# One core, hybrid attention model: order of loads, high parts and low parts around the exchange of the streamed operand in the last stage

## Chip, cores and metric

The kernel runs as one program on one core of a Trainium2 chip. The metric is the time of one execution on the device in microseconds, over several runs. Engines are named as in the profile: PE (matrix multiply), ACT (scalar), DVE (vector), POOL (GpSimd), SP (the queue that issues most of the transfers).

## What is computed

The reference is two blocks one after the other on a sequence of 1024 tokens with 1024 channels: the first with window attention, a bidirectional mLSTM and a mixture of experts, the second with an even and an odd layer and a last RMS norm. The change touches only the end of the odd layer and that norm:

```python
def odd_layer(x, norm_g, w_in, conv_w, w_out):
    ...
    y_c = y_c.reshape(Bn, S, C_WIDTH) * jax.nn.silu(g_c)
    y_d = short_gated_conv(d_b, d_c, d_x, conv_w) * jax.nn.silu(g_d)
    return x + jnp.concatenate([y_c, y_d], axis=-1) @ w_out
...
    return rmsnorm_2(h, final_norm)
```

The last product is y (1024 tokens x 2048) by w_out (2048 x 1024), in float32. The kernel splits each float32 operand into a high part (a cast to the matmul's format) and a low part (the rest), and adds three products of them.

## The kernel before

**Stages.** The stages follow one another in one program; each gives each engine its instructions in a fixed order, and an engine works them off in that order. Semaphores carry the dependences. The odd layer is phase_odd.

**Pairs and products.** The odd layer's projections and the last product run in *pairs* m: two tiles of 128 weight columns by 1024 channels against the tokens, done by a scheme with seven half-size products in place of eight (class Quarters). Product i of pair m is 12 matmuls: 4 slices of the contraction by high x high, high x low, low x high, each 128 x 128 by 512 columns. Pairs 0 to 39 serve the attention heads, 40 to 55 the convolution (PAIRS = 56), and 56 to 63 the last product. There the roles turn: the pieces of y are what is loaded as stationary weights (quarter_raw, quarter_hi, quarter_lo), and w_out is the operand that streams (odd_t_sum raw, odd_t_hi, odd_t_lo), seven pieces of 1 MB each. Four of the seven are sums that the kernel has made beforehand and stored (last_w_sums). Pairs 56 to 59 take chunk 0 of w_out, pairs 60 to 63 chunk 1. So the seven streamed pieces are exchanged twice, while pair 55 gives way to pair 56 and pair 59 to pair 60. Piece i can be overwritten once product i of the pair before is through.

**Who does what.** SP loads: four quarters of the weights of each pair (Quarters.load, part 0 three of them, part 1 the last; each waits until POOL has used the buffer), the operand's pieces (load_operand, waits for product i of the last pair of the chunk before), tiles of x (load_x), and it stores the rows of the result. POOL makes for each pair four sums of quarters and seven low parts, in the order sum 1, 2, 3, low 0 to 3, sum 4, low 4 to 6 (Quarters.pool, lines 3009, 3012, 3013, 3020 and 3002). ACT makes the high parts of the weights, four products ahead: hi(m, i) makes that of product 7m + i + 4 (line 2996), so hi(m, 2) is the one of (m, 6) and hi(m, 3) that of (m+1, 0). ACT also copies products 0, 1, 2 and 6 of a pair out of PSUM (copy, line 3106; for chunk 1 DVE does that, add, line 4991), and makes the operand's high parts (operand_hi, line 4445). DVE joins products 3, 4 and 5 to what was copied (join, line 3112) and makes the operand's low parts (operand_lo, line 4940).

**What PE waits for.** Quarters.multiply makes PE wait for the low part of the weights of that product, and besides:

```python
                if i == 2:
                    pe.wait_ge(self.copied, 4 * m + 1)
                if i == 3 and m >= 2:
                    pe.wait_ge(self.joined, 3 * (m - 2) + 3)
                if i == 4:
                    pe.wait_ge(self.copied, 4 * m + 3)
                if i == 6:
                    pe.wait_ge(self.joined, 3 * (m - 1) + 2)
```

So product 4 waits for the copy of product 2, and product 6 for the join of product 4. In pairs 56 and 60 each product waits for its operand low part too.

**The norm.** In pairs 61 to 63 the rows of the pair before are finished beside the products: ACT sums the squares, DVE makes the mean (mean), ACT the root (root), DVE the inverse and the scaling, SP the store. add_x adds the turned x.

## Time and profile before

| | us |
|---|---|
| median of 3 runs | 3244.09 |
| lowest, highest | 3243.22, 3247.24 |
| the profiled execution, its own time | 3243.6 |
| its span, first to last instruction | 3241.9 |
| mean granted clock of PE, share of full speed | 0.984 |

One execution was recorded by the hardware profiler. A row of a timeline gives start and length of an instruction in microseconds from the start of the span, and in brackets how long its engine sat idle before it and what released it ("issue" where the profile shows no releaser). The start of a matmul is measured and its end is modelled, so matmuls that follow one another overlap in the rows; the pace is read from start to start. The last stage, pairs 56 to 63, takes the last 180 us of the span.

### The profile page before, as it was taken

Reading aid. Unit: us, or ns where it says so; the run is one execution under the profiler, and the core shown is the slowest. Engines: PE = TensorE matmul, PEld = TensorE weight load, DVE = VectorE, ACT = ScalarE, POOL = GpSimd, SP = SyncE. Lnnn points to the kernel's source line nnn. Section 1 sums busy time; section 2 is a strip of 40 time slices with the busy share of each in tenths; the row PEclk is TensorE's granted clock in tenths of the full one; section 3 lists DMA queues with packets and bytes.
Section 4 is the critical chain, followed back from the end, with each engine's and each line's share of the span. In section 5 each row is a group of like instructions: output and inputs, shape, how many; then the busy total and the mean of one; then the engine's idle time right before and its main releaser. Section 6 shows DMA issues by size and latency. Waiting matters only on the chain. (4 is left out here: it accounts for less than half of the span.)

```text
span 3241.9 us, 43876 instructions
## 1 busy us (share of the span) xinstructions
PE 3104.1 (96%) x16242; PEld 2572.7 (79%) x16242; DVE 1707.5 (53%) x2457; ACT 1452.3 (45%) x2457; POOL 1683.6 (52%) x1096
## 2 busy tenths in 40 slices
PE   6989999889899989999999999999999999999998
PEld 4777887866788868788888788888888888888777
DVE  5366633854799876622523744444444444467544
ACT  5156313723677743333401555445455445333443
POOL 2331323042322249976643656556556556689886
PEclk8999999999899989999999999999999999999999
DMA  8230212173999952222432111111111111244553
GB/s 297 56 86 21 57 40 75 44 260 119 337 400 394 375 166 69 78 98 62 155 101 80 40 47 52 46 53 46 46 56 43 47 56 43 89 146 162 169 173 106
DMA packets 341492, 388.12 MB, mean 120 GB/s; under 512 B 29367, under 2 KB 297563, under 8 KB 335012
## 3 DMA queue, kind: packets, MB, share of 16 engines
q1 hardware_dynamic: 329374, 344.39, 31.7%
q0 software_dynamic: 4896, 16.78, 2.0%
q10 hardware_dynamic: 7014, 24.17, 1.9%
q8 instruction: 131, 2.15, 0.3%
q14 instruction: 77, 0.63, 0.1%
HBM read 313.73 MB, written 68.16 MB: 118 GB/s over the span
## 5 line engine op out<-in xcount | busy, mean ns | idle before, releaser
L3002 POOL TENSOR_TENSOR quarter_lo<-quarter_w_sums,quarter_hi 128x512 fp32r<-128x512 f32 x325 | 470.5, 1455 | 244.5 <-ACT quarter_hi L2996 242.1
L3002 POOL TENSOR_TENSOR quarter_lo<-quarter_raw,quarter_hi 128x512 fp32r<-128x512 f32 x244 | 355.0, 1455 | 280.2 <-ACT quarter_hi L2996 273.2
L3092 PE MATMUL odd_z<-odd_t_hi,quarter_hi 128*128 128x512 f32 x876 | 362.4, 414 | 4.3 <-POOL quarter_lo L3002 3.8
L2996 ACT CAST quarter_hi<-quarter_w_sums 128x512 fp32r<-128x512 f32 x325 | 202.4, 623 | 362.9 <-PE first_z L3094 172.5
L3092 PE MATMUL first_z<-odd_t_hi,quarter_hi 128*128 128x512 f32 x868 | 358.8, 413 | 6.1 <-issue 4.8
L3094 PE MATMUL odd_z<-odd_t_hi,quarter_lo 128*128 128x512 f32 x876 | 343.6, 392 | 0.0
L3093 PE MATMUL odd_z<-odd_t_lo,quarter_hi 128*128 128x512 f32 x876 | 342.1, 391 | 0.0
L3094 PE MATMUL first_z<-odd_t_hi,quarter_lo 128*128 128x512 f32 x868 | 339.8, 391 | 0.0
L3093 PE MATMUL first_z<-odd_t_lo,quarter_hi 128*128 128x512 f32 x868 | 338.3, 390 | 0.0
L2996 ACT CAST quarter_hi<-quarter_raw 128x512 fp32r<-128x512 f32 x244 | 151.5, 621 | 120.7 <-PE first_z L3094 55.8
L276 POOL TENSOR_TENSOR w_hi<-w_raw,zero_col 128x1024 fp32r<-128x1024 f32 x25 | 49.7, 1990 | 288.1 <-DMA w_raw<-in_w_in 98.0
L3092 PEld LDWEIGHTS odd_z<-odd_t_hi,quarter_hi 128*128 128x128 f32 x876 | 165.2, 189 | 36.7 <-POOL quarter_lo L3002 4.7
L3092 PEld LDWEIGHTS first_z<-odd_t_hi,quarter_hi 128*128 128x128 f32 x868 | 163.3, 188 | 38.1 <-issue 9.1
L3094 PEld LDWEIGHTS odd_z<-odd_t_hi,quarter_lo 128*128 128x128 f32 x876 | 164.8, 188 | 36.2
L3094 PEld LDWEIGHTS first_z<-odd_t_hi,quarter_lo 128*128 128x128 f32 x868 | 162.8, 188 | 35.8
L3093 PEld LDWEIGHTS odd_z<-odd_t_lo,quarter_hi 128*128 128x128 f32 x876 | 165.4, 189 | 30.1
L3093 PEld LDWEIGHTS first_z<-odd_t_lo,quarter_hi 128*128 128x128 f32 x868 | 163.6, 188 | 29.4
L4755 DVE SCALAR_TENSOR_TENSOR dil_biased<-const,odd_aux 128x128 f32<-128x128 f32 (+1 forms) x192 | 78.0, 406 | 192.4 <-PE odd_aux L4268 122.6
L3106 ACT ACTIVATE dil_set<-odd_z 128x512 f32<-128x512 f32 x112 | 90.7, 810 | 175.0 <-PE odd_z L3094 175.0
L3106 ACT ACTIVATE dil_set<-first_z 128x512 f32<-128x512 f32 x108 | 88.3, 818 | 166.6 <-PE first_z L3094 166.6
L4775 DVE COPY dil_p_t<-odd_aux 128x128 f32<-128x128 f32 (+1 forms) x192 | 67.7, 353 | 171.7 <-PE odd_aux L4285 151.7
L3009 POOL TENSOR_TENSOR quarter_w_sums<-quarter_raw 128x512 f32<-128x512 f32 x82 | 119.6, 1458 | 28.6 <-POOL quarter_lo L3002 13.3
(716 smaller groups left out, 7790.2 us busy)
## 6 DMA issues: line engine op xcount, KB each, us to landing
quarter_raw<-in_odd_w_in SPq DMA_DIRECT2D x224, 256.0 KB, 3.5
raw_gate<-in_w_gate SPq DMA_DIRECT2D x16, 2048.0 KB, 15.7
raw_up<-in_w_up SPq DMA_DIRECT2D x16, 2048.0 KB, 15.8
raw_down<-in_w_down SPq DMA_DIRECT2D x16, 2048.0 KB, 15.5
quarter_raw<-in_even_w_in SPq DMA_DIRECT2D x64, 256.0 KB, 3.3
start_w_mod<-in_w_mod SPq DMA_DIRECT2D x11, 1024.0 KB, 10.8
w_raw<-in_w_in SPq DMA_DIRECT2D x16, 512.0 KB, 3.8
mix_w_early<-in_w_mod SPq DMA_DIRECT2D x8, 1024.0 KB, 12.0
```

The source lines that it names most:

```text
L276: pool.tensor_tensor(w_hi[:, u], w_raw[:, u], zero_col[:, 0:1].to_broadcast([P, KT * P]).rearrange("p (k n) -> p k n", k=KT), ALU.add).the ...
L2996: act.copy(self.home(n)[0][:], self.source(m, i)).then_inc(self.hi_done, 1)
L3002: pool.tensor_tensor(lo[:], self.source(m, i), hi[:].bitcast(F32), ALU.subtract).then_inc(self.split, 1)
L3009: pool.tensor_tensor(sums[:, 0], a21, a22, ALU.add).then_inc(self.added, 1)
L3092: pe.matmul(to, w_hi[:, kt], t_hi[:, kt], start=(begins and kt == 0), stop=False, skip_group_check=True)
L3093: pe.matmul(to, w_hi[:, kt], t_lo[:, kt], start=False, stop=False, skip_group_check=True)
L3094: ins = pe.matmul(to, w_lo[:, kt], t_hi[:, kt], start=False, stop=(kt == KT // 2 - 1), skip_group_check=True)
L3106: act.activation(to[t][half], self.bank(m, i, banks, to), ACT.Copy, scale=scale).then_inc(self.copied, 1)
L4755: dve.scalar_tensor_tensor(out=biased[:, u % 2, 0:w], in0=dist, scalar=cst("slopes")[:, g * C_SLOTS + h:g * C_SLOTS + h + 1], in1=score[:, ...
L4775: dve.tensor_copy(p_t[:, u % 2, 0:w], turned[:, 0:w]).then_inc(free, 1)
```

## The change

The same instructions are issued with the same operands; only their order on SP, ACT and DVE differs. No instruction is added or removed. In the order of the diff:

- SP issues the load of the operand's sixth piece (load_operand(chunk, 5)) ahead of the first three weight quarters of the next pair, and no longer behind them, for both chunks.
- ACT, pairs 55 and 59: operand_hi(chunk, 0) stands ahead of the copy of product 2, and operand_hi(chunk, 1) to (chunk, 4) each behind hi(m, 2) to hi(m, 5); before, operand_hi(chunk, 0) to (chunk, 2) stood ahead of hi(m, 3) to hi(m, 5) and operand_hi(chunk, 3) behind them, and (chunk, 4) in the next pair.
- ACT, pair 56: operand_hi(0, 5) first, operand_hi(0, 6) ahead of the copy of product 2, and that copy ahead of hi(56, 1). Pair 60: operand_hi(1, 5), hi(60, 0), operand_hi(1, 6).
- DVE, pairs 55 and 59: operand_lo(chunk, 0), (chunk, 1), (chunk, 2) stand ahead of the joins of products 3, 4, 5; before they stood behind them. Pair 56: operand_lo(0, 6) ahead of the join of product 3. Pair 60: operand_lo(1, 5) ahead of the addition of product 2.
- DVE, pairs 61 to 63: the addition of product 2 (add(m, 2)) stands ahead of mean and of the first add_x.

```diff
--- before.py
+++ after.py
@@ -4187,8 +4187,8 @@
                     load(m)
                     for i in range(5):
                         load_operand(0, i)
+                    load_operand(0, 5)
                     load(m + 1, (0,))
-                    load_operand(0, 5)
                     load_operand(0, 6)
                     load(m + 1, (1,))
                     sp.wait_ge(x_stored, 16)
@@ -4204,8 +4204,8 @@
                     load(m + 4)
                     for i in range(5):
                         load_operand(1, i)
+                    load_operand(1, 5)
                     load(m + 5, (0,))
-                    load_operand(1, 5)
                     load_operand(1, 6)
                     load(m + 5, (1,))
                     load_x(4)
@@ -4570,14 +4570,13 @@
                         hi(m, 0)
                         copy(m, 1)
                         hi(m, 1)
+                        if c == KT - 1:
+                            operand_hi(0, 0)
                         copy(m, 2)
-                        hi(m, 2)
-                        for i in (3, 4, 5):
+                        for i in (2, 3, 4, 5):
+                            hi(m, i)
                             if c == KT - 1:
-                                operand_hi(0, i - 3)
-                            hi(m, i)
-                        if c == KT - 1:
-                            operand_hi(0, 3)
+                                operand_hi(0, i - 1)
                         copy(m, 6)
                         hi(m, 6)
                         if c == 0:
@@ -4604,15 +4603,14 @@
                     m = PAIRS
                     for u in range(2):
                         act.wait_ge(w_piece_stored[u], 16 * (PIECES // 2))
+                    operand_hi(0, 5)
                     copy(m, 0)
                     hi(m, 0)
-                    operand_hi(0, 4)
                     copy(m, 1)
+                    operand_hi(0, 6)
+                    copy(m, 2)
                     hi(m, 1)
-                    operand_hi(0, 5)
-                    copy(m, 2)
                     hi(m, 2)
-                    operand_hi(0, 6)
                     hi(m, 3)
                     hi(m, 4)
                     hi(m, 5)
@@ -4627,20 +4625,20 @@
                             store_y(KO - 1, conv_acc)
                         copy(m, 1)
                         hi(m, 1)
+                        if last:
+                            operand_hi(1, 0)
                         copy(m, 2)
-                        hi(m, 2)
-                        for i in (3, 4, 5):
+                        for i in (2, 3, 4, 5):
+                            hi(m, i)
                             if last:
-                                operand_hi(1, i - 3)
-                            hi(m, i)
-                        if last:
-                            operand_hi(1, 3)
+                                operand_hi(1, i - 1)
                         copy(m, 6)
                         hi(m, 6)
                     m += 1
-                    for i in range(7):
-                        if i < 3:
-                            operand_hi(1, i + 4)
+                    operand_hi(1, 5)
+                    hi(m, 0)
+                    operand_hi(1, 6)
+                    for i in range(1, 7):
                         hi(m, i)
                     for m in range(m + 1, PAIRS + OUT_PAIRS):
                         q = place(m - 1)[1]
@@ -4961,15 +4959,11 @@
                     for c in range(1, KT):
                         for m in (CONV_AT + 2 * c, CONV_AT + 2 * c + 1):
                             split = c == KT - 1 and m % 2
-                            join(m, 3)
+                            for i in (3, 4, 5):
+                                if split:
+                                    operand_lo(0, i - 3)
+                                join(m, i)
                             if split:
-                                operand_lo(0, 0)
-                            join(m, 4)
-                            if split:
-                                operand_lo(0, 1)
-                            join(m, 5)
-                            if split:
-                                operand_lo(0, 2)
                                 operand_lo(0, 3)
                             if m % 2 == 0:
                                 convolve(c, 0, 1, 2, 3)
@@ -5003,10 +4997,9 @@
                         return dve.scalar_tensor_tensor(out=x, in0=x, scalar=row_rstd[:, j:j + 1], in1=gain_rows[:, cols], op0=ALU.mult, op1=ALU.mult)
 
                     m = PAIRS
-                    operand_lo(0, 4)
-                    operand_lo(0, 5)
+                    for i in (4, 5, 6):
+                        operand_lo(0, i)
                     join(m, 3)
-                    operand_lo(0, 6)
                     join(m, 4)
                     join(m, 5)
                     gate_conv(KT - 1)
@@ -5016,17 +5009,18 @@
                         if turned is not None:
                             quarters.wait_pair(dve, PAIRS + turned)
                             add_x(2 * turned)
+                        if last:
+                            operand_lo(1, 0)
                         join(m, 3)
                         if last:
-                            operand_lo(1, 0)
+                            operand_lo(1, 1)
                         join(m, 4)
-                        if last:
-                            operand_lo(1, 1)
                         if turned is not None:
                             add_x(2 * turned + 1)
+                        if last:
+                            operand_lo(1, 2)
                         join(m, 5)
                         if last:
-                            operand_lo(1, 2)
                             operand_lo(1, 3)
                     m += 1
                     dve.wait_ge(x_added, 8)
@@ -5034,8 +5028,8 @@
                     add(m, 0)
                     operand_lo(1, 4)
                     add(m, 1)
+                    operand_lo(1, 5)
                     add(m, 2)
-                    operand_lo(1, 5)
                     operand_lo(1, 6)
                     join(m, 3)
                     join(m, 4)
@@ -5049,11 +5043,11 @@
                         quarters.wait_pair(dve, m - 1)
                         add(m, 0)
                         add(m, 1)
+                        add(m, 2)
                         mean(2 * q + 2, js)
                         if turned is not None:
                             dve.wait_ge(x_added, 4 * turned)
                             add_x(2 * turned)
-                        add(m, 2)
                         inverse(q + 1, js)
                         join(m, 3)
                         if q == 0:
```

## Rows read from the trace of the kernel before

**Rows 1.** The page's table of busy time by engine, over the whole span.

```profile
PE 3104.1 (96%) x16242; PEld 2572.7 (79%) x16242; DVE 1707.5 (53%) x2457; ACT 1452.3 (45%) x2457; POOL 1683.6 (52%) x1096
```

**Rows 2.** Busy time by windows; columns: stretch, length, engines with counts, clock, DMA.

```profile
3060.80:3086.02 25.22, 20.70 (x84) 15.29 (x84) 16.55 (x10) 15.04 (x18) 23.73 (x13) 1.00 0.52 167
...
3147.10:3172.50 25.40, 19.71 (x84) 15.53 (x84) 18.38 (x12) 11.63 (x13) 25.01 (x13) 1.00 0.54 176
```

**Rows 3.** Timeline of PE; columns: start, length, engine, line, operation, [idle before <-releaser].

```profile
3052.05 0.39 PE L3092 MATMUL odd_z<-odd_t_hi,quarter_hi 128*128 128x512 f32 x1
...
3061.60 0.47 PE L3092 MATMUL first_z<-odd_t_hi,quarter_hi 128*128 128x512 f32 x1 [0.80 <-issue]
...
3075.79 0.47 PE L3092 MATMUL first_z<-odd_t_hi,quarter_hi 128*128 128x512 f32 x1 [1.29 <-ACT last_rows L3106]
...
3086.02 0.50 PE L3092 MATMUL odd_z<-odd_t_hi,quarter_hi 128*128 128x512 f32 x1 [1.49 <-POOL quarter_lo L3002]
...
3138.72 0.39 PE L3092 MATMUL odd_z<-odd_t_hi,quarter_hi 128*128 128x512 f32 x1
...
3150.14 0.47 PE L3092 MATMUL first_z<-odd_t_hi,quarter_hi 128*128 128x512 f32 x1 [3.09 <-issue]
...
3172.50 0.50 PE L3092 MATMUL odd_z<-odd_t_hi,quarter_hi 128*128 128x512 f32 x1 [2.35 <-POOL quarter_lo L3002]
```

**Rows 4.** Timeline of ACT in pair 55.

```profile
3047.30 0.61 ACT L2996 CAST quarter_hi<-quarter_w_sums 128x512 fp32r<-128x512 f32 x1
3049.53 0.60 ACT L3106 ACTIVATE dil_set<-odd_z 128x512 f32<-128x512 f32 x1 [1.61 <-PE odd_z L3094]
3050.02 0.61 ACT L2996 CAST quarter_hi<-quarter_raw 128x512 fp32r<-128x512 f32 x1
3052.37 1.91 ACT L4445 CAST odd_t_hi<-odd_t_sum 128x2048 fp32r<-128x2048 f32 x1 [1.73 <-DMA odd_t_sum<-in_odd_w_out]
```

**Rows 5.** Timeline of ACT in pair 59.

```profile
3136.20 0.60 ACT L3106 ACTIVATE last_rows<-odd_z 128x512 f32<-128x512 f32 x1 [1.61 <-PE odd_z L3094]
...
3137.56 1.91 ACT L4445 CAST odd_t_hi<-odd_t_sum 128x2048 fp32r<-128x2048 f32 x1 [0.25 <-DMA odd_t_sum<-in_odd_w_out]
```

**Rows 6.** Timeline of POOL in pairs 55 and 59.

```profile
3050.71 1.29 POOL L3002 TENSOR_TENSOR quarter_lo<-quarter_raw,quarter_hi 128x512 fp32r<-128x512 f32 x1
3052.17 1.30 POOL L3009 TENSOR_TENSOR quarter_w_sums<-quarter_raw 128x512 f32<-128x512 f32 x1 [0.17 <-POOL quarter_lo L3002]
...
3054.86 3.34 POOL L3013 TENSOR_TENSOR quarter_w_sums<-quarter_raw 128x512 f32<-128x512 f32 x1
...
3137.39 1.30 POOL L3002 TENSOR_TENSOR quarter_lo<-quarter_raw,quarter_hi 128x512 fp32r<-128x512 f32 x1 [1.37 <-ACT quarter_hi L2996]
```

**Rows 7.** DVE's operand low parts: tile view (min/median/max ns), then timeline.

```profile
L4940 DVE TENSOR_TENSOR odd_t_lo<-odd_t_sum,odd_t_hi x14: 2292/2780/3374, 3054.3 to 3162.5; 128x2048 fp32r<-128x2048 f32 x14
...
3054.31 2.74 DVE L4940 TENSOR_TENSOR odd_t_lo<-odd_t_sum,odd_t_hi 128x2048 fp32r<-128x2048 f32 x1 [1.37 <-ACT odd_t_hi L4445]
...
3139.53 2.77 DVE L4940 TENSOR_TENSOR odd_t_lo<-odd_t_sum,odd_t_hi 128x2048 fp32r<-128x2048 f32 x1
```

**Rows 8.** Windows of 5 us of PE: stretch, length, busy, granted clock, DMA.

```profile
3150.00:3155.00 5.00, 4.55 (x19) 1.00 0.75 248
...
3170.00:3175.00 5.00, 2.65 (x8) 0.79 0.50 147
3175.00:3180.00 5.00, 5.00 (x23) 0.87 0.21 62
```

**Rows 9.** Tile view of the operands' raw buffers: issue to landing.

```profile
DMA to landing us min/median/max: 5.2/7.3/8.9
```

**Rows 10.** Timelines of DVE and ACT in pair 61, around mean and root.

```profile
3183.49 0.69 DVE L4991 TENSOR_TENSOR last_rows<-odd_z,last_rows 128x512 f32<-128x512 f32 x1 [1.39 <-PE odd_z L3094]
...
3184.13 1.28 ACT L4602 ACT_TABLE_LOAD   x1
...
3186.21 0.62 ACT L2996 CAST quarter_hi<-quarter_raw 128x512 fp32r<-128x512 f32 x1 [0.58 <-PE first_z L3094]
```

## Prediction, made before the changed kernel ran

> **What bounds the kernel now.** First the page's busy table [rows 1]: the matmul engine is busy 96% of the span, so nearly every microsecond in which it waits comes back in the time. The change touches only the last stage, so the next view is the busy time by windows around the two places where the streamed operand is exchanged [rows 2]. I call them E1 (first exchange, operand of chunk 0, pairs 55 and 56) and E2 (second exchange, chunk 1, pairs 59 and 60). PE is busy 20.70 of 25.22 us in the one and 19.71 of 25.40 us in the other, while POOL is busy 23.73 and 25.01. The reader is to see that POOL, not PE, is full there.
>
> PE's own timeline gives the beats [rows 3]. I write (m,i) for product i of pair m. (55,4) starts at 3052.05, (56,0) at 3061.60, (57,0) at 3086.02; (59,4) at 3138.72, (60,0) at 3150.14 after 3.09 us of idling, (61,0) at 3172.50 after 2.35 us behind POOL's low part. Without a wait a product takes 12 matmuls of 0.2267 us, 2.72 us (start to start in the timeline), and a pair 19.04.
>
> ACT's timeline shows what the change will run into [rows 4, 5]. In E1 ACT copies (55,2) at 3049.53, makes the high part of (55,6) at 3050.02, and then idles 1.73 us until operand 0 has landed, so the first operand high part starts at 3052.37. In E2 the copy stands at 3136.20 and the operand high part at 3137.56; there the wait is 0.25.
>
> POOL's and DVE's timelines show why the low parts are scarce [rows 6, 7]. A POOL instruction takes 1.29 us alone (3050.71, 3052.17), and 3.34 us from the moment at which DVE makes the operand's low part beside it (3054.86). A low part on DVE takes 2.29 us at the least, 2.78 in the median. So while both have work queued, one POOL instruction and one operand low part pass in some 3.3 us.
>
> **The change part by part.**
>
> *operand_hi(c,0) ahead of the copy of (m,2), m = 55 and 59.* ACT works in program order, and nothing lets operand 0 land sooner: its load stands where it stood in SP's queue. So ACT has its last high part, of (55,5), done at 3047.9 (3047.30 + 0.61), stands still until 3052.37, works 1.9 us on the operand, and copies (55,2) at 3054.2 instead of 3049.53. Two things are queued behind it. (a) PE's (m,4) needs that copy (Quarters.multiply): (55,4) starts at 3054.95, not 3052.05, +2.9. In E2 the copy comes at 3139.4 and (59,4) at 3140.05, +1.3. (b) The high part of (m,6) follows the copy: 3054.7 instead of 3050.02, and 3139.9 instead of 3136.7 (0.5 behind the start of the copy, as in E1). POOL's low part of (m,6) needs it, and POOL's sums for pair m+1 stand behind that in POOL's order.
>
> *What (b) costs.* Before, POOL had its low part of (55,6), L3009 and L3012 through before DVE's first operand low part began at 3054.31 [rows 6, 7]; in E2 the low part of (59,6) and L3009. Now all five instructions from that low part to the low part of (56,0), on which PE waits, run beside DVE's operand low parts, which come every 2.7 us (an operand of 1 MB each product) and so always stand ready. Five by 3.3 is 16.5: (56,0) starts at 3054.3 + 16.5 = 3070.8, not 3061.60, and (60,0) at 3139.5 + 16.5 = 3156.0, not 3150.14. The ends: if 1.29 and 2.29 simply add up, 17.9 us, so 3072.2 and 3157.4; if POOL gets through one of the five alone, 14.5 us, so 3068.8 and 3154.0.
>
> The row behind 3.3 is POOL's 3.34 against 1.29 [rows 6]. On this the Trainium skill ("SBUF — State Buffer", Reading the diagram under the two separate sides) says that the port pair shared by DVE and GpSimd is an exclusive lock, held for a whole instruction by whichever began first, the other blocking fully. By that rule the pair would cost the full sum, 1.29 + 2.29 = 3.58, and five 17.9 us, 1.4 us more in each place than by the row. It speaks against this change, which pushes POOL's work under DVE's.
>
> *From there to the next pair.* Once PE stands so long, POOL gets ahead, and pair 56 runs at PE's own pace: 19.04 plus 0.5 for (56,1), where POOL's next low part ends. Check on POOL by the sum of both engines' work, which is what filled E1 before: 7 x 2.29 + 13 x 1.29 = 32.8 us calculated from 3054.3 to the low part of (57,0), 31.7 measured (it ended just ahead of 3086.02). With three POOL instructions more it is 3.9 more: 3089.9. PE's walk gives 3070.8 + 19.5 = 3090.3, so PE's is the later. E2: two instructions more, 2.6: 3175.1; PE's walk 3156.0 + 19.5 = 3175.5.
>
> *The clock.* After the 2.35 us stall at 3172.50 the granted clock fell to the lower level of the two (1.2 for 2.4 GHz): 0.79 and 0.87 in two slices of 5 us [rows 8], a loss of 5 x 0.21 + 5 x 0.13 = 1.7 us. After the 3.09 us stall at 3150.14 it stayed at 1.00. So a stall may or may not bring a fall. The new stalls ahead of (56,0) and (60,0) are some 7.7 us each (3063.1 to 3070.8, 3148.3 to 3156.0), more than twice either, so I take one fall at each, 1.7 us. In E2 it takes the place of the one that is there, as (61,0) no longer waits.
>
> *Sum.* E1: 3090.3 + 1.7 = 3092.0 against 3086.0, +6.0. E2: 3175.5 + 1.7 = 3177.2 against 3172.5 + 1.7 = 3174.2, +3.0. Together +9.0. Bounds: 2 us less or 1.4 us more at each place; zero to one fall more or less.
>
> *Load of operand 5 ahead of the load of pair m+1.* It leaves SP when product 5 is through, and no longer behind that load's waits. Operand 6 now stands behind load (57, part 0), which waits for the low part of (56,0), 3070.8. It leaves at 3071.2, lands by 3077 (ACT's wait for operand 0 ended 5.3 us after 3047.1, and the slowest landing was 8.9 us [rows 9]: 3080), and its high and low part take 1.9 + 3.3: 3082 to 3085. (56,6) isn't due before 3070.8 + 0.5 + 16.3 = 3087.6. Nothing, by 2.6 us at the worst; without PE's own lateness it would be the next limit. Operand high parts 4, 5 and 6 earlier, copy (56,2) ahead of the high part that waited for POOL: they take away a wait of 1.29 us at (56,4) [rows 3], but that lies inside the walk above and is already counted by it.
>
> *Low parts ahead of joins.* A join of 0.7 us is put behind a low part. join (55,3) ends about 3057.6; PE asks for it again only at (56,1). (56,6) needs join (56,4), behind join (56,3) and the low part of operand 6: 1.3 us after 3085 at worst, 3086.3, inside the 3087.6. Nothing.
>
> *Third addition ahead of the mean, pairs 61 to 63.* The addition waits for product 2: DVE adds at 3183.49 [rows 10]. The mean comes 0.7 us later, at 3184.2, and ACT's root could otherwise begin its table load at 3184.13: 0.1 to 0.2 us late. The next high part on ACT starts at 3186.21, 0.6 us after the root. Nothing at all, at most 0.5 if that cover went at each pair.
>
> **The rivals.**
> *R1, the backlog is smaller.* The clock doesn't fall anew, and POOL wins back part of its lateness while PE waits. Lower end: only the stalls of (a), 2.9 + 1.3 = 4.2; upper end the port sum alone, 3.9 + 2.6 = 6.5. For it: the clock stayed up after 3.09 us. Against: POOL is busy 94% and 98% of these windows, there is hardly room to win back. Time 3248.3 to 3250.6.
> *R2, it is heavier.* The full sum at each place, 2 x 1.4 = 2.8, and perhaps one more fall, 1.7: +11.8 to +13.5, 3256 to 3258.
> *R3, faster.* ACT isn't held, since operand 0 is there in time, and only the earlier operands count: the waits of 1.29 at (56,4), 1.49 at (57,0) and 2.35 at (61,0) go, with the fall behind it, 1.7: -6.8, 3237.3. It decides at the landing: operand 0 must be there before 3047.9 in E1 and 3134.6 in E2, 4.5 and 2.9 us earlier than ACT's waits show [rows 4, 5], with nothing moved ahead of it on SP.
> *R4, no effect.* POOL's lateness is absorbed wholly and the stall at (m,4) is taken out of the later ones: 3244. Against it stands the same 94 to 98%. I put it together with R1.
>
> **How the numbers follow.** The profiled run took 3243.6 us (span 3241.9 and 1.7 around it); the median of the runs is 3244.1, 0.5 above. Likeliest: 3243.6 + 9.0 + 0.5 = 3253.1, say 3253, own range 3250.6 to 3256. Chances: forecast 0.60, R1 with R4 0.25, R2 0.08, R3 0.07. 0.2% is 6.5 us, about what a measurement of this kernel can tell from no change: "same" runs from 3237.6 to 3250.6. That gives faster 0.07, same 0.25, slower 0.68. The range reaches into R1 and through R2: 3247 to 3258.
>
> **What would show it.** ACT's timeline: idle for about 4.5 us ahead of operand_hi(0,0) and 3 us ahead of operand_hi(1,0), copy of (55,2) at 3054. POOL: the low part of (55,6) beginning at 3055.4, five instructions of about 3 us on end. PE: a new stall of 2.9 us at (55,4), about 8 us before (56,0), none at (61,0). The clock: a slice under 1.0 in E1. It is wrong if operand 0 lands earlier than in the profile shown, if POOL's five pass at near 1.3 us, or if PE's stall ahead of (56,0) stays under 3 us.

## The result, and the profile after

The changed kernel takes 3250.78 us (median of 14 runs, 3248.77 to 3254.8); the kernel before, run beside it, 3243.38 (14 runs, 3240.99 to 3247.24). The ratio is 1.0025, with an interval of 1.0017 to 1.0033: slower by 5.5 to 10.7 us. The profiled execution took 3251.13 us (span 3249.4), 7.5 more than the profiled one of before (3243.6, span 3241.9). One of the 12 runs of e3_hi_late, below, took 6291.19 us, nearly twice as long as the others, and is left out of its median and ratio.

The busy line of the page hardly moves, and PE has 2.1 us more to show than in [rows 1], which fits the few more matmuls that ran at the lower clock:

```profile
PE 3106.2 (96%) x16242; PEld 2575.3 (79%) x16242; DVE 1704.6 (52%) x2457; ACT 1453.3 (45%) x2457; POOL 1681.2 (52%) x1096
```

So the loss is mostly idle time. PE's timeline, columns as in [rows 3], shows where:

```profile
3055.55 0.47 PE L3092 MATMUL odd_z<-odd_t_hi,quarter_hi 128*128 128x512 f32 x1 [2.35 <-ACT dil_set L3106]
...
3071.61 0.77 PE L3092 MATMUL first_z<-odd_t_hi,quarter_hi 128*128 128x512 f32 x1 [7.32 <-issue]
...
3092.53 0.39 PE L3092 MATMUL odd_z<-odd_t_hi,quarter_hi 128*128 128x512 f32 x1
...
3146.45 0.47 PE L3092 MATMUL odd_z<-odd_t_hi,quarter_hi 128*128 128x512 f32 x1 [1.22 <-ACT last_rows L3106]
...
3160.61 0.77 PE L3092 MATMUL first_z<-odd_t_hi,quarter_hi 128*128 128x512 f32 x1 [5.42 <-issue]
...
3181.60 0.50 PE L3092 MATMUL odd_z<-odd_t_hi,quarter_hi 128*128 128x512 f32 x1
```

These are (55,4), (56,0), (57,0), (59,4), (60,0) and (61,0). Before, (55,4) and (59,4) waited for nothing, (56,0) 0.80 and (60,0) 3.09. Against that, the waits of 1.29 at (56,4), 1.49 at (57,0) and 2.35 at (61,0) are gone.

ACT, on which (55,4) waits (it answers to [rows 4, 5]):

```profile
3048.29 0.61 ACT L2996 CAST quarter_hi<-quarter_w_sums 128x512 fp32r<-128x512 f32 x1
3053.01 1.90 ACT L4445 CAST odd_t_hi<-odd_t_sum 128x2048 fp32r<-128x2048 f32 x1 [4.11 <-DMA odd_t_sum<-in_odd_w_out]
3054.82 0.59 ACT L3106 ACTIVATE dil_set<-odd_z 128x512 f32<-128x512 f32 x1
3055.31 0.61 ACT L2996 CAST quarter_hi<-quarter_raw 128x512 fp32r<-128x512 f32 x1
...
3143.91 1.91 ACT L4445 CAST odd_t_hi<-odd_t_sum 128x2048 fp32r<-128x2048 f32 x1 [2.97 <-DMA odd_t_sum<-in_odd_w_out]
3145.73 0.58 ACT L3106 ACTIVATE last_rows<-odd_z 128x512 f32<-128x512 f32 x1
```

The copy of (55,2) needs nothing that isn't there, yet it starts at 3054.82 and not about 3050.5, since the instruction ahead of it in ACT's program waits 4.11 us for a transfer.

POOL, on which (56,0) waits though the row says "issue" (it answers to [rows 6]); the first four rows are E1's, the last five E2's:

```profile
3055.99 2.40 POOL L3002 TENSOR_TENSOR quarter_lo<-quarter_raw,quarter_hi 128x512 fp32r<-128x512 f32 x1 [4.41 <-ACT quarter_hi L2996]
3058.57 3.12 POOL L3009 TENSOR_TENSOR quarter_w_sums<-quarter_raw 128x512 f32<-128x512 f32 x1 [0.17 <-POOL quarter_lo L3002]
...
3064.94 3.31 POOL L3013 TENSOR_TENSOR quarter_w_sums<-quarter_raw 128x512 f32<-128x512 f32 x1
3068.33 3.19 POOL L3002 TENSOR_TENSOR quarter_lo<-quarter_raw,quarter_hi 128x512 fp32r<-128x512 f32 x1
...
3146.89 2.41 POOL L3002 TENSOR_TENSOR quarter_lo<-quarter_raw,quarter_hi 128x512 fp32r<-128x512 f32 x1 [4.52 <-ACT quarter_hi L2996]
3149.47 3.14 POOL L3009 TENSOR_TENSOR quarter_w_sums<-quarter_raw 128x512 f32<-128x512 f32 x1 [0.17 <-POOL quarter_lo L3002]
3152.75 3.14 POOL L3012 TENSOR_TENSOR quarter_w_sums<-quarter_w_sums,quarter_raw 128x512 f32<-128x512 f32 x1
3155.86 3.31 POOL L3013 TENSOR_TENSOR quarter_w_sums<-quarter_raw 128x512 f32<-128x512 f32 x1
3159.24 1.27 POOL L3002 TENSOR_TENSOR quarter_lo<-quarter_raw,quarter_hi 128x512 fp32r<-128x512 f32 x1
```

POOL idles 4.4 us, then needs 2.4 us for the first and 3.1 to 3.3 us for each of the next, which took 1.3 alone. Five pass in E1 from 3055.99 to 3071.52, and (56,0) starts 0.1 behind. In E2 the fifth runs alone (1.27).

**A ruler for small differences.** The stages ahead of the change hold the same instructions in every kernel here, and yet one and the same row there starts anywhere between 3040.30 us (e2_act_only) and 3045.43 us (e11_early_before) in the 14 profiles, a spread as wide as most effects below. So each kernel is also measured from this row as an anchor: the start of DVE's multiplication `conv_prod` for channel block 7, which lies ahead of what the edits touch. Before:

```profile
3042.06 1.23 DVE L4906 TENSOR_TENSOR conv_prod<-dil_set 128x1024 f32<-128x1024 f32 x1 [2.71 <-ACT dil_set L3106]
```

After:

```profile
3043.04 1.23 DVE L4904 TENSOR_TENSOR conv_prod<-dil_set 128x1024 f32<-128x1024 f32 x1 [2.71 <-ACT dil_set L3106]
```

The tail (span less anchor) is 3241.9 - 3042.06 = 199.84 before and 3249.4 - 3043.04 = 206.36 after: +6.5 of the 7.5 us arise in the tail, and 1.0 lies ahead of it. PE's first transposition of x behind (57,0) cuts the tail in two: it starts at 3091.62 before and 3097.98 after, so E1 costs 6.36 - 0.98 = +5.4, and the rest, E2, +1.1. A tail has chance in it too: the clock alone moves it by some 1.6 us (see e7_norm_only).

### The profile page after: what moved, and what is told of

The parts are those of the page before. It is cut to its first block and busy times, and to the rows that moved or that the text cites. A ratio compares the mean times of both kernels' runs of the same rounds, so it can differ in the third digit from the quotient of the medians.

```text
span 3249.4 us, 43876 instructions
## 1 busy us (share of the span) xinstructions
PE 3106.2 (96%) x16242; PEld 2575.3 (79%) x16242; DVE 1704.6 (52%) x2457; ACT 1453.3 (45%) x2457; POOL 1681.2 (52%) x1096
## 5 line engine op out<-in xcount | busy, mean ns | idle before, releaser
L3009 POOL TENSOR_TENSOR quarter_w_sums<-quarter_raw 128x512 f32<-128x512 f32 x82 | 121.4, 1481 | 28.2 <-POOL quarter_lo L3002 13.5
```

What stands on the lines that cost most here:

```text
L3009: pool.tensor_tensor(sums[:, 0], a21, a22, ALU.add).then_inc(self.added, 1)
```

## The experiments

Twelve kernels, each compared with the kernel before on the same chip. Not all groups ran on one chip, and the median of the kernel before is 3240.93 to 3242.20 us in them; so kernels are set against each other by ratio and tail, not by median. "Tail" is the change of the tail against before's 199.84 us, from one profile each, and "E1" its part up to that transposition. The ratio is that of the runs, with its interval.

| kernel | ratio | tail, us | of it E1 |
|---|---|---|---|
| after | 1.0025 (1.0017 to 1.0033) | +6.5 | +5.4 |
| e2_act_only | 1.0033 (1.0020 to 1.0046) | +8.1 | +5.0 |
| e3_hi_late | 1.0019 (1.0011 to 1.0028) | +4.0 | +3.1 |
| e4_copy_late | 1.0002 (0.9993 to 1.0011) | 0.0 | 0.0 |
| e1_act_back | 1.0002 (0.9993 to 1.0011) | -1.3 | +0.2 |
| e12_both_back | 1.0008 (0.9999 to 1.0017) | +2.1 | +1.7 |
| e6_dve_only | 1.0005 (0.9996 to 1.0014) | +0.3 | -0.2 |
| e8_psum_after | 0.9985 (0.9976 to 0.9995) | -7.6 | -1.2 |
| e9_psum_before | 0.9965 (0.9952 to 0.9978) | -12.4 | -6.1 |
| e10_early_after | 1.0017 (1.0007 to 1.0027) | +2.9 | +2.7 |
| e11_early_before | 1.0000 (0.9990 to 1.0009) | -0.4 | -0.4 |
| e5_sp_only | one run | -0.1 | 0.0 |
| e7_norm_only | one run | -1.8 | 0.0 |

### Is it the one move on ACT? (e2_act_only)

The kernel before, with nothing changed but the place of one instruction in each exchange.

```diff
                         hi(m, 1)
+                        if c == KT - 1:
+                            operand_hi(0, 0)
                         copy(m, 2)
                         hi(m, 2)
                         for i in (3, 4, 5):
-                            if c == KT - 1:
+                            if c == KT - 1 and i > 3:
                                 operand_hi(0, i - 3)
```

(and the same for chunk 1 in pair 59.)

> The kernel before, with one move: in pairs 55 and 59 ACT makes the high part of operand piece 0 ahead of the copy of product 2 and ahead of the high part of product 6. Theory (this move is the loss): product 4 starts about 2.5 us late in pair 55 and 1.2 us late in pair 59, POOL's low part of product 6 starts 4.5 and 3.2 us late, PE idles 5 to 8 us ahead of products (56,0) and (60,0), one slice under 1.00 of granted clock behind each; time +5 to +8 us over before. Rival (the low parts ahead of the joins and the load of piece 6 behind POOL are the loss): time within 1.5 us of before.

Measured: median 3251.43 us. PE's timeline:

```profile
3052.64 0.47 PE L3092 MATMUL odd_z<-odd_t_hi,quarter_hi 128*128 128x512 f32 x1 [2.18 <-ACT dil_set L3106]
...
3066.89 0.77 PE L3092 MATMUL first_z<-odd_t_hi,quarter_hi 128*128 128x512 f32 x1 [5.81 <-issue]
...
3157.62 0.76 PE L3092 MATMUL first_z<-odd_t_hi,quarter_hi 128*128 128x512 f32 x1 [5.90 <-issue]
...
3180.39 0.50 PE L3092 MATMUL odd_z<-odd_t_hi,quarter_hi 128*128 128x512 f32 x1 [0.60 <-POOL quarter_lo L3002]
```

The stalls of the changed kernel are all there ((59,4), not shown, waits 1.18 us). This single move carries the whole loss, in the tail even 1.6 us more than the whole change. That excess arises in E2 (+3.1 against +1.1), and most of it is the clock: behind (60,0) it stayed low for 14 matmuls, and for 8 in the changed kernel (about 0.2 us lost on each). A wait of 0.60 is left at (61,0) besides, and one of 0.87 at (57,0).

### Which of the two things queued behind the wait? (e3_hi_late, e4_copy_late)

Behind the waiting instruction stand the copy of (m,2), for PE, and the high part of (m,6), for POOL. Each of the next two kernels delays one of them and leaves the other where it was. e3_hi_late:

```diff
                         copy(m, 2)
+                        if c == KT - 1:
+                            operand_hi(0, 0)
                         hi(m, 2)
```

(Here and in the next, operand_hi(0, 0) leaves its old place further down, as above, and the same is done for chunk 1.)

> The kernel before, with the high part of operand piece 0 put between the copy of product 2 and the high part of product 6 in pairs 55 and 59. PE isn't held at product 4; POOL gets its low part of product 6 late. Theory (POOL's lateness is the price, the stall at product 4 only comes on top of idling that is there anyway): (56,0) starts 8 to 9 us late as in the changed kernel, and the time is +4 to +7 us. Rival (the stall of PE at product 4 is the price): within 1.5 us of before.

e4_copy_late:

```diff
-                        copy(m, 2)
                         hi(m, 2)
+                        if c == KT - 1:
+                            operand_hi(0, 0)
+                        copy(m, 2)
```

> The kernel before, with the order: high part of product 6, high part of operand piece 0, copy of product 2, in pairs 55 and 59. POOL isn't held; PE is held at product 4 by 2.5 and 1.2 us. Theory (POOL's lateness is the price): the stall is taken out of the later waits for POOL, (56,0) starts 1 to 2 us late, (57,0) not at all, time 0 to +2 us. Rival (the stall at product 4 is the price): +3.5 us or more.

Measured: e3_hi_late, median 3248.32. PE doesn't wait at product 4, but at product 0 of the next pair in both exchanges:

```profile
3067.29 0.76 PE L3092 MATMUL first_z<-odd_t_hi,quarter_hi 128*128 128x512 f32 x1 [6.16 <-issue]
...
3156.64 0.77 PE L3092 MATMUL first_z<-odd_t_hi,quarter_hi 128*128 128x512 f32 x1 [5.78 <-issue]
```

The time is as expected, the beat isn't: on the ruler (56,0) comes 4.9 us later than before, not 8 to 9. ACT's and DVE's rows show why:

```profile
3061.33 0.62 ACT L2996 CAST quarter_hi<-quarter_w_sums 128x512 fp32r<-128x512 f32 x1 [4.00 <-POOL quarter_w_sums L3009]
...
3063.78 5.57 DVE L4944 TENSOR_TENSOR odd_t_lo<-odd_t_sum,odd_t_hi 128x2048 fp32r<-128x2048 f32 x2 [3.08 <-ACT odd_t_hi L4445]
```

ACT needs POOL's first sum before it comes to operand_hi(0, 2), so POOL's lateness holds ACT, ACT holds DVE, and while DVE idles POOL passes L3012 and L3013 alone, in 1.26 and 1.27 us.

e4_copy_late, median 3242.89:

```profile
3054.24 0.47 PE L3092 MATMUL odd_z<-odd_t_hi,quarter_hi 128*128 128x512 f32 x1 [2.67 <-ACT dil_set L3106]
...
3085.31 0.50 PE L3092 MATMUL odd_z<-odd_t_hi,quarter_hi 128*128 128x512 f32 x1 [1.50 <-POOL quarter_lo L3002]
...
3141.64 0.77 PE L3092 MATMUL odd_z<-odd_t_hi,quarter_hi 128*128 128x512 f32 x1 [3.45 <-ACT last_rows L3106]
...
3173.35 0.50 PE L3092 MATMUL odd_z<-odd_t_hi,quarter_hi 128*128 128x512 f32 x1 [2.33 <-POOL quarter_lo L3002]
```

Here PE stands 2.67 and 3.45 us at product 4 (1.2 was expected for the second; operand 0 landed some 2.2 us later there, on the ruler, than in before, after and e2_act_only), loses some clock as well behind the second, and the tail is the same to 0.1 us. The stalls of 0.80 and 3.09 at (56,0) and (60,0) have gone in exchange, and those at (57,0) and (61,0) are what they were: POOL sets those beats, and PE's wait is spent out of time that it would have spent waiting for POOL anyway. So the lateness of POOL is the price and the late copy alone is free.

The two don't add up, though: 4.0 and 0.0 alone, 8.1 together. Most of the 4.1 us between them stands in POOL's rows. Its five instructions take 13.7 and 13.8 us in e2_act_only and 12.1 and 12.2 in e3_hi_late, since DVE pauses for two of them in e3_hi_late and for one, L3009, in e2_act_only; and in E1 they begin 0.5 us later on the ruler. So on top of a late POOL a late copy isn't free. This is read from the rows; no kernel here tests it by itself.

### Is it the port that DVE and POOL share? (e8_psum_after, e9_psum_before)

The operand's low part takes its second input from a PSUM bank, not from SBUF, in four instructions of 512 columns. The operand low parts then hold other numbers, so these two kernels leave out the right result and serve only for the time.

```diff
-                        dve.tensor_tensor(odd_tokens[i][1][:], odd_sums[i][:], odd_tokens[i][0][:].bitcast(F32), ALU.subtract).then_inc(operand_split, 1)
+                        for k in range(KT // 2):
+                            ins = dve.tensor_tensor(odd_tokens[i][1][:, k], odd_sums[i][:, k], aux[:, 0, :], ALU.subtract)
+                        ins.then_inc(operand_split, 1)
```

On the changed kernel:

> The changed kernel, in which DVE makes each operand low part by four instructions of 512 columns that subtract a bank of PSUM from the raw piece in place of its high part: some 2.5 us as before, but with one input from SBUF in place of two (the low parts hold other numbers, so the output isn't the reference's). Theory (a port that DVE's second SBUF input shares with POOL slows POOL): the five POOL instructions ahead of (56,0) take 1.3 us each again, the stall ahead of (56,0) falls from 7.3 us to under 1 us, that ahead of (60,0) too, no fall of the clock; -8 to -14 us against the changed kernel. Rival (POOL is slowed by something else that goes on then, the transfers or ACT): POOL stays at 3.1 to 3.3 us, time within 2 us of the changed kernel.

On the kernel before:

> The kernel before with the same edit of the operand low parts (same numbers left out). Theory: POOL at 1.3 us, the waits of PE for POOL in pairs 56, 57, 60 and 61 shrink to waits for the operand's own parts, -5 to -10 us against before; e8_psum_after is 0 to 4 us slower than this one, the stalls at (55,4) and (59,4), 2.4 and 1.2 us, and no more. Rival: time within 2 us of before.

Measured on the changed kernel: 3236.29 us (the kernel before on that chip: 3241.21). The POOL rows that answer to those of E1 above, and DVE's low parts in the tile's view (duration in ns, minimum, median and maximum):

```profile
3056.56 1.29 POOL L3002 TENSOR_TENSOR quarter_lo<-quarter_raw,quarter_hi 128x512 fp32r<-128x512 f32 x1 [4.29 <-ACT quarter_hi L2996]
3058.02 1.29 POOL L3009 TENSOR_TENSOR quarter_w_sums<-quarter_raw 128x512 f32<-128x512 f32 x1 [0.17 <-POOL quarter_lo L3002]
...
3060.72 1.30 POOL L3013 TENSOR_TENSOR quarter_w_sums<-quarter_raw 128x512 f32<-128x512 f32 x1
3062.10 1.30 POOL L3002 TENSOR_TENSOR quarter_lo<-quarter_raw,quarter_hi 128x512 fp32r<-128x512 f32 x1
...
L4939 DVE TENSOR_TENSOR odd_t_lo<-odd_t_sum,odd_aux x56: 673/678/689, 3055.5 to 3161.3; 128x512 fp32r<-128x512 f32 x56
```

DVE has a little more to do than before (four take 2.48 us on end, against 2.29 for the one alone) and yet POOL passes its five in 6.8 us and not 15.5. PE doesn't wait at (56,0) or (60,0). POOL still idles 4.29 us for ACT: that wait is harmless once the instructions behind it are short. Tail -14.1 us against the changed kernel. That the edit also makes four short instructions of one isn't the reason: if POOL still had to wait for a short one, its rows would be up to 0.68 us longer, and they are 1.29 to 1.31. The Trainium skill ("SBUF — State Buffer", Who interferes with whom) says that a DVE instruction with two inputs in SBUF contends with a GpSimd one that reads SBUF, and that one with at most one such input, outside the two-port modes, doesn't; the trace agrees, 3.12 to 3.31 us against 1.29 to 1.31.

On the kernel before the same edit gives 3230.07 us, 11.1 less where 5 to 10 were expected, and between the two stand 6.2 us of the medians (4.8 of the tails) where 0 to 4 were expected: two misses. All of the 4.8 lies in E1. There a part of the loss is left when the port is free: e8_psum_after waits 2.23 at (55,4), with a fall of the clock behind it that its expectation excluded (its next rows start 0.43 us apart), and 1.07 at (56,2). The first of these is the late copy. It was free in e4_copy_late, where POOL was the bound.

### Would it be harmless if piece 0 were there? (e10_early_after, e11_early_before)

The load of operand 0 leaves SP ahead of the second half of pair m's load.

```diff
-                    load(m)
-                    for i in range(5):
+                    load(m, (0,))
+                    load_operand(0, 0)
+                    load(m, (1,))
+                    for i in range(1, 5):
                         load_operand(0, i)
```

(and the same for chunk 1.) On the changed kernel:

> The changed kernel, with the load of operand piece 0 put ahead of the last weight quarter of pairs 56 and 60 on SP, so that it leaves as soon as product 0 of pair 55 or 59 is through. Theory (the loss hangs on ACT standing still until piece 0 has landed): ACT's wait ahead of it falls from 4.1 us to about 2 in pair 55 and from 3.0 to about 1.5 in pair 59, the stall of PE at (55,4) from 2.35 to under 0.5, POOL's low part of product 6 comes some 2 and 1.5 us earlier; -2 to -5 us against the changed kernel. Rival (the transfers are the limit, and the same bytes come in another order): piece 0 lands at the same time, within 1 us.

On the kernel before:

> The kernel before with the same earlier load of piece 0. Theory (the summed work of POOL and DVE fills the exchange, and POOL is at work alone until the first low part anyway): the low part of piece 0 comes 1 to 2 us earlier, POOL's sums beside it take 3.1 to 3.3 us in place of 1.3, and nothing is gained: within 1.5 us of before. Rival (the landing of piece 0 is the limit of the exchange): -2 to -4 us.

Measured: e10_early_after 3246.97 us, tail 3.6 us shorter than the changed kernel's. ACT, then PE at (55,6) and (56,0):

```profile
3050.05 1.91 ACT L4449 CAST odd_t_hi<-odd_t_sum 128x2048 fp32r<-128x2048 f32 x1 [1.36 <-DMA odd_t_sum<-in_odd_w_out]
...
3058.62 0.47 PE L3092 MATMUL odd_z<-odd_t_hi,quarter_hi 128*128 128x512 f32 x1 [0.19 <-DVE dil_set L3112]
...
3068.95 0.77 PE L3092 MATMUL first_z<-odd_t_hi,quarter_hi 128*128 128x512 f32 x1 [7.33 <-issue]
```

ACT's operand high part 0 starts 2.7 us earlier on the ruler, and the stall at (55,4) is gone ((55,6) waits 0.19). Yet (56,0) still waits 7.33, since POOL's low part of (55,6) begins at 3053.05, DVE's first operand low part at 3052.00, and all five run beside them (2.41, 3.39, 3.15, 3.31, 3.19). So an earlier operand gives back about half of the loss and leaves the rest. In the kernel before the same early load gives nothing (3241.81): POOL's L3012 grows from 1.29 to 3.18 us, (56,0) waits 3.11, and what comes early for DVE comes at POOL's expense. With ACT's order as before, the landing of operand 0 isn't the limit; POOL's work beside DVE's is.

### The parts costed at nothing (e1_act_back, e12_both_back, e6_dve_only, e5_sp_only, e7_norm_only)

e1_act_back is the changed kernel with ACT's order in pairs 55 and 59 put back, but for operand high part 4, which stays in these pairs.

```diff
-                        if c == KT - 1:
-                            operand_hi(0, 0)
                         copy(m, 2)
-                        for i in (2, 3, 4, 5):
-                            hi(m, i)
+                        hi(m, 2)
+                        for i in (3, 4, 5):
                             if c == KT - 1:
-                                operand_hi(0, i - 1)
+                                operand_hi(0, i - 3)
+                            hi(m, i)
+                        if c == KT - 1:
+                            operand_hi(0, 3)
+                            operand_hi(0, 4)
```

> The changed kernel, with operand high part 0 back behind the copy of product 2 and the high part of product 6 in pairs 55 and 59 (and parts 1 to 3 ahead of the high parts 3 to 5 as before; part 4 stays in pairs 55 and 59, all else stays changed). Theory: the loss goes, -6 to -10 us against the changed kernel; against before 0 to -4 us, since pieces 5 and 6 are there earlier and the waits at (56,4), (57,0) and (61,0) shrink. Rival (the other moves cost too): +3 us or more over before.

Measured: 3242.34 us. The loss is gone, and in its place are two stalls that are nothing in the kernel before and 0.2 us in the changed one:

```profile
3062.35 0.49 PE L3092 MATMUL odd_z<-odd_t_hi,quarter_hi 128*128 128x512 f32 x1 [3.44 <-DVE dil_set L3112]
...
3147.78 0.57 PE L3092 MATMUL odd_z<-odd_t_hi,quarter_hi 128*128 128x512 f32 x1 [2.02 <-DVE last_rows L3112]
```

This is product 6 of pairs 55 and 59. In Quarters.multiply it waits for join (m,4), and DVE now does two operand low parts ahead of that join. The second of them, and the join:

```profile
3058.84 2.77 DVE L4942 TENSOR_TENSOR odd_t_lo<-odd_t_sum,odd_t_hi 128x2048 fp32r<-128x2048 f32 x1
3061.53 0.68 DVE L3112 SCALAR_TENSOR_TENSOR dil_set<-odd_z,dil_set 128x512 f32<-128x512 f32 x1
```

Both are paid out of later waits (those at (56,0), (57,0), (60,0) and (61,0) are gone; 1.52 at (56,4) and 2.71 at (60,4) are left), so the tail isn't lengthened by them.

Is the pure DVE part good or bad, then? e12_both_back puts the low parts back behind the joins in e1_act_back, and e6_dve_only makes the DVE part alone on the kernel before.

```diff
                             for i in (3, 4, 5):
+                                join(m, i)
                                 if split:
                                     operand_lo(0, i - 3)
-                                join(m, i)
```

> The changed kernel with two things back as before: in pairs 55 and 59 operand high part 0 stands behind the copy of product 2 and the high part of product 6, and the low parts 0 to 2 stand behind the joins of products 3 to 5. What is left of the change: the load of piece 5, high parts 4 to 6 earlier, the copy of (56,2), low part 6 ahead of join 3 in pair 56, the third addition. Theory (the profile of e1_act_back: PE idled 3.44 and 2.02 us at product 6 for the join of product 4, which stood behind low part 1, and the granted clock fell behind it): both stalls and both falls go, time -2 to -5 us against before. Rival (POOL's work beside the low parts sets the end of the pair anyway): within 1 us of before.

> The kernel before with DVE's part of the change alone (low parts ahead of joins in pairs 55 and 59, low part 6 ahead of join 3, low part (1,5) ahead of the third addition, third addition ahead of the mean). Theory: PE idles some 3.3 us at (55,6) and 2 us at (59,6), waiting for the join of product 4 behind low part 1; part of it comes out of the later waits for POOL; time 0 to +4 us over before. Rival (these moves cost nothing, as predicted): no stall at product 6, within 1 us.

Measured: e12_both_back 3244.92 (before on that chip: 3241.21), tail +2.1, where a gain of 2 to 5 us was expected: a miss, though the interval of its ratio still reaches 0.9999. The stalls at product 6 did go. But PE now waits 3.56 us at (56,4) and 3.60 at (60,4), for POOL's low parts, each with a fall of the clock behind it:

```profile
3077.35 0.50 PE L3092 MATMUL first_z<-odd_t_hi,quarter_hi 128*128 128x512 f32 x1 [3.56 <-issue]
...
3165.75 0.47 PE L3092 MATMUL first_z<-odd_t_hi,quarter_hi 128*128 128x512 f32 x1 [3.60 <-POOL quarter_lo L3002]
```

The reason stands in DVE's timeline:

```profile
3060.17 15.96 DVE L4942 TENSOR_TENSOR odd_t_lo<-odd_t_sum,odd_t_hi 128x2048 fp32r<-128x2048 f32 x5
```

Five operand low parts run end to end, since operands 4 to 6 are there earlier, and POOL gets one instruction in between two of them. So operands that come earlier seem to be a load on the port as well; no kernel here takes that part away alone. e6_dve_only is at 3242.77, tail +0.3: the same stall at product 6 (3.43 and 2.18 us), paid out of later waits again.

SP's part alone (load of operand 5 ahead of the load of the next pair), and the third addition ahead of the mean alone:

```diff
+                    load_operand(0, 5)
                     load(m + 1, (0,))
-                    load_operand(0, 5)
```

> The kernel before with SP's part of the change alone (piece 5 loaded ahead of the weight quarters of the next pair). Theory: piece 5 is there earlier than ACT comes to it, piece 6 waits for nothing that comes later than before; PE's timeline in pairs 55 to 61 as before within 0.5 us. Rival: the weight quarters behind piece 5 come late for POOL's sums of pair 57 or 61, +1 us or more.

```diff
                         add(m, 1)
+                        add(m, 2)
                         mean(2 * q + 2, js)
...
-                        add(m, 2)
                         inverse(q + 1, js)
```

> The kernel before with the third addition of pairs 61 to 63 ahead of the mean alone. Theory: the mean comes at most 0.3 us later than ACT could have begun its root, the next high part on ACT isn't moved, PE's timeline as before, end within 0.3 us. Rival: a wait of PE of 0.2 us or more in each of the pairs 61 to 63.

e5_sp_only took 3246.03 in its one run, but its tail is -0.1 and PE's waits are those of the kernel before to 0.02 us (0.79, 1.28, 1.51, 3.10, 2.34): 2.5 us lie ahead of the anchor. e7_norm_only took 3241.34, tail -1.8 where the expectation allowed 0.3, but the moved addition has no share in it: the gain stands ahead of the first moved addition. In pair 60 the same wait of 3.09 us was followed by a fall of the clock, in the kernel before it was not, and (61,0) then waited only 0.91 and kept the clock, where the kernel before lost about 1.6 us. From (61,0) to the end it is 67.8 us, as in e2_act_only and e3_hi_late, in which the addition stands where it was. PE by windows (granted clock behind its busy time), in e7_norm_only:

```profile
3149.00:3154.00 5.00, 4.40 (x13) 0.66 0.72 237
3171.00:3176.00 5.00, 4.19 (x18) 1.00 0.53 157
```

and in the kernel before:

```profile
3149.00:3154.00 5.00, 3.56 (x15) 1.00 0.70 218
3171.00:3176.00 5.00, 3.50 (x9) 0.69 0.53 157
```

A difference of this size in a tail may be chance.

## Why the prediction was right, step by step

The direction and the place were right: slower, by an instruction on ACT that waits for a transfer. 3253.0 was forecast and 3250.78 measured, inside the range, and at the lower edge of the likeliest case's own range (3250.6). Set against the profiled run, +9.0 was forecast and +7.5 came, of which +6.5 in the tail. The 0.5 us that the sum adds for the median rest on three runs and were chance: over 14 runs the median of the kernel before is 3243.38, 0.2 below the profiled run. Measured beats below have the shift of the stage taken off (0.98 in E1, 6.36 in E2, from the ruler), so that they stand beside the forecast ones.

- **ACT stands still.** Forecast about 4.5 us and 3, copy at 3054.2. Measured 4.11 and 2.97, copy at 3053.84. Right.
- **(55,4) and (59,4).** Forecast 3054.95 and 3140.05; measured 3054.57 and 3140.09. Right in size. But the sum gave these steps no price of their own only because POOL's chain came later, and e4_copy_late confirms it: 2.67 and 3.45 us of PE's waiting cost nothing in the tail.
- **POOL's five instructions.** For E1 16.5 us and 3070.8 were forecast; (56,0) came at 3070.63. That it fits to 0.2 us is partly luck, as two errors cancel: the sum counts the five from DVE's start at 3054.3, though they can begin only with POOL's low part (3055.01 measured, 0.7 later; 3055.4 stands in the prediction's own list of signs), and they took 15.5 us and not 16.5, since the first of them met only the rest of a low part (2.40). The mechanism is shown: e3_hi_late keeps most of the loss with POOL's delay alone (+4.0 of +6.5), e8_psum_after removes POOL's slowness, and PE's waits at (56,0) and (60,0), with the port free. The port's full sum of 3.58 us for each pair, R2's ground, is not borne out: 3.1 to 3.3 us stand in the rows.
- **The same in E2.** This is the term that was mis-sized. Forecast 3156.0, measured 3154.25, so 14.8 us from the prediction's start at 3139.5 and not 16.5 (the five themselves began 1.0 later and took 13.6), near the lower end that the prediction named (one of five alone). DVE's timeline shows why the fifth had the port:

```profile
3155.28 2.76 DVE L4938 TENSOR_TENSOR odd_t_lo<-odd_t_sum,odd_t_hi 128x2048 fp32r<-128x2048 f32 x1
3165.38 0.69 DVE L4985 TENSOR_TENSOR last_rows<-first_z,last_rows 128x512 f32<-128x512 f32 x1 [7.34 <-PE first_z L3094]
3165.99 2.28 DVE L4938 TENSOR_TENSOR odd_t_lo<-odd_t_sum,odd_t_hi 128x2048 fp32r<-128x2048 f32 x1
```

  The claim that operand low parts "always stand ready" fails here. In E2 the fifth one stands in DVE's program behind add (60,0), which needs the very product (60,0) that PE can't begin. DVE idles 7.34 us, and POOL has the port. In E1 nothing like it stands between.
- **From there at PE's own pace.** Forecast 21.2 us with the clock's fall, in both; measured 20.92 (3071.61 to 3092.53) and 20.99 (3160.61 to 3181.60). Right: the waits at (56,4), (57,0) and (61,0) are gone.
- **One fall of the clock at each place.** Right, in this profile. The clock in the two windows, 0.56 and 0.59, is a mixture of the lower level (0.50) and the full one:

```profile
3071.00:3076.00 5.00, 4.38 (x12) 0.56 0.69 234
3160.00:3165.00 5.00, 4.39 (x12) 0.59 0.89 274
```

  From 3071.61 to 3075.17 eight matmuls take 3.56 us instead of 1.81: 1.75 us, against 1.7 forecast. Behind (61,0) there is none.
- **Sum by places.** E1 +5.4 (forecast +6.0), E2 +1.1 (forecast +3.0). Nearly all of what is missing is the 1.8 us in E2.
- **Load of operand 5, third addition: nothing.** Right. e5_sp_only has the tail of the kernel before. At the addition ACT's next high part stands 0.58 us idle, as in [rows 10].
- **Low parts ahead of joins: nothing.** The time was right, the reason wrong. The prediction said that PE asks for these joins again only in pair 56, and overlooked that product 6 of the same pair waits for join 4. With ACT's order put back this costs 3.44 and 2.02 us at (55,6) and (59,6). In the changed kernel PE comes to (55,6) and (59,6) so late that only 0.2 us of it is seen: the cover was another stall, which the prediction never named.
- **R1** (4.2 to 6.5 in all, no fall of the clock) has the measured tail, +6.5, as its upper end, but that is a coincidence: its way there was another, and the clock fell twice. **R3** needed operand 0 before ACT asks. e10_early_after brings it most of the way (1.36 us of the wait left) and is still slower than the kernel before, so its gain would hardly have come from the landing alone: the rival left out that DVE's low parts would be early too. **R4** is excluded by the interval.

What stays open: how much of any one tail is the clock's chance, and whether the earlier operands 4 to 6, part of the change, cost something by themselves: e12_both_back has them and +2.1 us, e1_act_back has them and -1.3.

## What to carry to other kernels

Ask of an instruction that waits for a transfer what stands behind it in its engine's program. The first victim (here PE's next product) may be free by itself because another engine is the bound, while a second one, that feeds the bound, carries the price: give each its own experiment, and don't expect the two to add up. Where DVE and POOL both read pairs of SBUF operands at the exchange of data, count their work as one queue, and know that bringing one engine's data earlier can make the other later. Here taking one input off the port was worth more (12.4 us of the tail) than any order of the same instructions that was tried.

## What the runs showed of the hardware

- A POOL instruction of 1.29 us and a DVE low part of 2.29 us that meet pass together in 3.1 to 3.4 us, somewhat less than their sum of 3.58, and they take turns one for one (in e12_both_back five low parts on end take 15.96 us, 3.2 each). With one DVE input in PSUM neither is longer than alone.
- The fall of TensorE's clock is no function of the stall alone: behind the same wait of 3.09 us at (60,0) the kernel before keeps 1.00 and e7_norm_only falls. Where it fell it lasted for about 6 to 14 matmuls of 0.43 us instead of 0.23, so 1.2 to 2.8 us.
- SP's load of 1 MB that left 2.5 us earlier on the ruler (3044.86 in e10_early_after, 3047.59 in the changed kernel) let ACT begin 2.7 us earlier. From 3044 to 3050 the DMA engines were busy 0.25 of the time in the changed kernel and 0.66 in e10_early_after; from 3050 to 3056 they were full in both (1.05 and 1.06).
